# A third use for a spare weight place, and expert 30 in 4 MB transfers, in a mixture-of-experts block

## The reference

```python
def moe_ffn(xn, w_router, b_router, w_mlp1, b_mlp1, w_mlp2, b_mlp2):
    ...
    top_val, top_idx = lax.top_k(logits, TOP_K)
    gate = jax.nn.softmax(top_val, axis=-1)
    ...
    def expert_block(args):
        xb, e = args
        hdn = xb @ w_mlp1[e] + b_mlp1[e]
        glu = jnp.minimum(hdn[:, :D_FF], SWIGLU_LIMIT)
        lin = jnp.clip(hdn[:, D_FF:], -SWIGLU_LIMIT, SWIGLU_LIMIT)
        act = glu * jax.nn.sigmoid(SWIGLU_ALPHA * glu) * (lin + 1.0)
        return act @ w_mlp2[e] + b_mlp2[e]
    ...
    return jnp.einsum('tk,tkd->td', gate.astype(y.dtype), y).reshape(bsz, s, d)
```

## Time and profile before

| | |
|---|---|
| median of 3 runs | 1119.99 us (1119.98 to 1119.99) |
| profiled execution, own time | 1121.66 us |
| its span | 1119.8 us |
| PE busy | 1073.4 us, 96% of the span |
| DMA share of the span (SP's queue) | 93.2% |
| mean granted TensorE clock | 0.995 |
| moved | 439.15 MB, 392 GB/s over the span |
| items | 33 |
| 4 MB loads | 72 |

### The profile page before, as it was taken

One profiled execution on the slowest core, in us unless ns is written; L12 is line 12 of the kernel. 1 busy time (PEld: TensorE's weight loads), 2 busy tenths in 40 slices (PEclk: granted clock), 3 DMA queues, 4 the chain that ended last, 5 costly groups with the idle time before them and its releaser, 6 DMA issues.

```text
span 1119.8 us, 14338 instructions
## 1 busy us (share of the span) xinstructions
PE 1073.4 (96%) x5327; PEld 471.7 (42%) x5328; DVE 382.2 (34%) x852; ACT 247.1 (22%) x346; POOL 3.0 (0%) x12
## 2 busy tenths in 40 slices
PE   8999999999999999999889999999988889998996
PEld 8888888533333333333333333333333333332332
DVE  5987787422232222222222222222222222222223
ACT  5745674311111111110111111111111111111112
POOL 0000000000000000000000000000000000000000
PEclk9999999999999999999999999999999999999999
DMA  9755488999999999999999999999999999999996
GB/s 331 238 164 170 154 273 363 424 419 422 428 427 434 429 431 434 430 429 431 431 433 404 432 431 431 431 431 431 431 431 431 433 431 434 434 433 433 423 424 265
DMA packets 38309, 439.15 MB, mean 392 GB/s; under 512 B 5292, under 2 KB 5480, under 8 KB 22440
## 3 DMA queue, kind: packets, MB, share of 16 engines
q1 hardware_dynamic: 37776, 437.26, 93.2%
q10 hardware_dynamic: 504, 1.47, 0.5%
HBM read 437.67 MB, written 1.05 MB: 392 GB/s over the span
## 4 chain that ended last, share of the span: by engine, by line
PE 70%; DMA 26%; DVE 2%; ACT 2%; issue 0%; DVEq 0%; SPq 0%; PEldq 0%; ACTq 0%
PE bank L1162 29%; PE bank L1217 15%; DMA late_slots<-in_w_mlp_dram 14%; DMA ring<-in_w_mlp_dram 11%; PE bank L821 9%; PE bank L1064 4%; PE bank L815 2%; PE bank L1103 2%; PE bank L983 2%; PE bank L1031 2%; PE bank L1087 1%; ACT xn L716 1%; PE bank L1154 1%; DMA xs<-in_x_dram 1%; PE bank L1080 0%
## 5 line engine op out<-in xcount | busy, mean ns | idle before, releaser
L1162 PE MATMUL bank<-ring,xn 128*64 128x512 f32 x1232 | 280.0, 602 | 18.3 <-DMA ring<-in_w_mlp_dram 18.2
L1162 PE MATMUL bank<-late_slots,xn 128*64 128x512 f32 x880 | 197.9, 596 | 12.6 <-DMA late_slots<-in_w_mlp_dram 12.6
L1162 PEld LDWEIGHTS bank<-ring,xn 128*64 128x64 f32 x1232 | 85.1, 138 | 179.5 <-issue 152.4
L1217 PE MATMUL bank<-ring,smo 128*64 128x512 f32 x624 | 138.3, 595 | 0.0
L728 ACT ACTIVATE xn<-bank 128x512 f32<-128x512 f32 x33 | 19.7, 598 | 436.6 <-PE bank L1162 436.6
L1162 PEld LDWEIGHTS bank<-late_slots,xn 128*64 128x64 f32 x880 | 59.9, 136 | 126.6 <-issue 105.4
L1730 DVE SCALAR_TENSOR_TENSOR moe_y_lo<-bank,st,moe_y_hi 128x512 fp32r<-128x512 f32 x33 | 24.8, 751 | 235.5 <-ACT moe_y_hi L735 235.5
L1217 PE MATMUL bank<-late_slots,smo 128*64 128x512 f32 x416 | 92.1, 595 | 0.0
L1714 DVE TENSOR_SCALAR xn<-xn 128x512 f32<-128x512 f32 x33 | 14.1, 427 | 190.8 <-ACT xn L728 190.8
L1217 PEld LDWEIGHTS bank<-ring,smo 128*64 128x64 f32 x624 | 43.0, 137 | 81.0 <-issue 81.0
L735 ACT ACTIVATE moe_y_hi<-bank,st 128x512 fp32r<-128x512 f32 x33 | 22.7, 688 | 243.2 <-PE bank L1217 243.2
(11 more groups left out here) (278 smaller groups left out, 871.8 us busy)
## 6 DMA issues: line engine op xcount, KB each, us to landing
ring<-in_w_mlp_dram SPq DMA_DIRECT2D x43, 4096.0 KB, 37.6
late_slots<-in_w_mlp_dram SPq DMA_DIRECT2D x29, 4096.0 KB, 35.5
ring<-in_w_mlp_dram SPq DMA_DIRECT2D x28, 2048.0 KB, 14.8
late_slots<-in_w_mlp_dram SPq DMA_DIRECT2D x14, 2048.0 KB, 16.3
ring<-in_w_in_dram SPq DMA_DIRECT2D x22, 1024.0 KB, 5.6
late_slots<-in_w_mlp_dram SPq DMA_DIRECT2D x8, 1024.0 KB, 35.5
ring<-in_w_branch_dram SPq DMA_DIRECT2D x4, 1024.0 KB, 5.0
ring<-in_w_out_dram SPq DMA_DIRECT2D x4, 1024.0 KB, 7.0
```

The source lines that it names most:

```text
L1162: last = mm(B[4 + u][g * C:(g + 1) * C, :], xgT[:, k % 4, k // 4, :], by_group(held[k // 2][0][:, k % 2, u * FF:(u + 1) * FF], g), start=F ...
L1217: last = mm(B[7][g * C:(g + 1) * C, :], actT[:, j, h * C:(h + 1) * C], held[4 + h][0][:, j // 2, (j % 2) * D + g * N:(j % 2) * D + (g + 1) ...
```

## The change

`once` is now used three times, by chunks 5, 16 and 27 (`ONCE`). `place_of` counts the ten other places past them. The sequence of loads therefore goes round eleven places up to chunk 27: chunks 11 to 37 wait for the chunk eleven before them (each e of the new loop has its `freed` chunks and loads m = freed + 11), chunk 27's room is not loaded again, and from chunk 38 on each waits for the chunk ten before it, as before. The ten places shift by two numbers against the chunks. `QUADS` is 6 to 30 instead of 6 to 29, so that expert 30 comes in three 4 MB transfers instead of six of 2 MB. The matmuls are the same, on other addresses.

```diff
-QUADS = range(ROUND + 1, E - 2)
+QUADS = range(ROUND + 1, E - 1)
...
+ONCE = (CHUNKS - 1, CHUNKS - 1 + PLACES + 1, CHUNKS - 1 + 2 * (PLACES + 1))
+EXTRA_LAST = ONCE[-1]
...
+def place_of(m):
+
+    return None if m in ONCE else (m - sum(o < m for o in ONCE)) % PLACES
...
-            after = sp.value_load(first_item[0:1, 1:2], min_val=1, max_val=ITEMS - 1)
-            for i in range(CHUNKS - 1):
-                m = PLACES + 1 + i
-                if m != HALVED:
-                    wait_freed(after, i)
-                load(m // CHUNKS, m % CHUNKS, i)
...
-                        load(e - c + (m + PLACES) // CHUNKS, (m + PLACES) % CHUNKS, (m - 1) % PLACES, pieces(m + PLACES))
+                        load(e - c + (m + PLACES) // CHUNKS, (m + PLACES) % CHUNKS, (m - len(ONCE)) % PLACES, pieces(m + PLACES))
...
-                        load_quad(e + 1 if i == 1 else e + 2, (i // 2 + 2) % 3, (m - 2) % PLACES)
-
-            for e in range(1, ROUND + 1):
+                        load_quad(e + 1 if i == 1 else e + 2, (i // 2 + 2) % 3, (m - 1 - len(ONCE)) % PLACES)
+
+            for e in range((EXTRA_LAST + CHUNKS - 1) // CHUNKS):
+                after = sp.value_load(first_item[0:1, e + 1:e + 2], min_val=1, max_val=ITEMS - 1)
+                for i in range(CHUNKS):
+                    freed = CHUNKS * e + i
+                    m = freed + PLACES + (freed < EXTRA_LAST)
+                    if freed == EXTRA_LAST:
+                        continue
+                    if m // CHUNKS not in QUADS:
+                        if m != HALVED:
+                            wait_freed(after, i)
+                        load(m // CHUNKS, m % CHUNKS, place_of(m))
+                    elif m % 2:
+                        wait_freed(after, i)
+                        load_quad(m // CHUNKS, m % CHUNKS // 2, place_of(m - 1))
+
+            for e in range((EXTRA_LAST + CHUNKS - 1) // CHUNKS, ROUND + 1):
                 refill(e, e, CHUNKS, e + 2 in QUADS, e + 1 in QUADS)
```

More of the change, by code:

```diff
@@ L109, in constants @@
     return c
+ONCE = (CHUNKS - 1, CHUNKS - 1 + PLACES + 1, CHUNKS - 1 + 2 * (PLACES + 1))
+EXTRA_LAST = ONCE[-1]
+assert all(CHUNKS * e > EXTRA_LAST + PLACES - 2 for e in QUADS)
+def place_of(m):
+    return None if m in ONCE else (m - sum(o < m for o in ONCE)) % PLACES
 def landings():
@@ L116, in landings @@
         e, i = m // CHUNKS, m % CHUNKS
-        if m == CHUNKS - 1:
-            table.append(None)
+        place = place_of(m)
+        if place is None:
+            table.append((None, ONCE.index(m) + 1))
             continue
-        place = m if m < CHUNKS else (m - 1) % PLACES
         if e in QUADS and i % 2:
@@ L1122, in chunks @@
             def chunks(e):
-                return [(places[(CHUNKS * e + i - 1) % PLACES], place_landed[landing[CHUNKS * e + i][0]],
-                         landing[CHUNKS * e + i][1] * 16) for i in range(CHUNKS)]
+                held = []
+                for m in range(CHUNKS * e, CHUNKS * (e + 1)):
+                    place, count = landing[m]
+                    held.append((once[:, :, :] if place is None else places[place_of(m)],
+                                 once_landed if place is None else place_landed[place], count * 16))
+                return held
             def chunks_in_round(c, r):
@@ L1140, in chunks_in_round @@
                             assert 0 < need <= past[-1]
-                    held.append((places[(CHUNKS * c + i - 1) % PLACES], place_landed[place],
+                    held.append((places[place_of(CHUNKS * (ROUND + c) + i)], place_landed[place],
                                  r * (16 * step) + 16 * (last - step * len(at))))
@@ L1222, in _ @@
             with pe.Fori(0, after_first) as i:
-                item(i, [(places[n], place_landed[n], 16) for n in range(CHUNKS - 1)] + [(once[:, :, :], once_landed, 16)])
+                item(i, chunks(0))
             last_first = pe.value_load(first_item[0:1, E - 1:E], min_val=1, max_val=ITEMS - 1)
```

## The result

The changed kernel takes 1121.81 us (median of 15 runs, 1120.95 to 1122.78); the kernel before took 1119.71 beside it (15 runs, 1118.76 to 1120.84). The ratio is 1.0017, 95% interval 1.001 to 1.0024: 2.1 us slower. That is inside the range, 1118.4 to 1121.9, but a change of -0.1 us was forecast. The profiled execution took 1121.84, span 1119.9.

The account below looks back on a forecast made before the run. PE was taken to wait for weights, loading being slower by 3.2 us an expert. -1.8 (extra place) + 1.7 (expert 30) = -0.1 us took the profiled 1121.66 to 1121.5, less 1.67 to 1119.9; range 1118.4 to 1121.9.

Parts of the forecast that it names:

- What bounds the kernel: Over most experts: PE waits for weights, since loading is slower than PE by 3.2 us an expert.
- a shift of the stream carries through: From early loads to the end: 1.8 us gained early stays, as landings hold PE before and after the two-item expert.
- The extra place, -1.8: At chunks 16 and 17: earlier issue keeps the DMA engines from running dry, gaining 1.7 + 0.1 = 1.8 us.
- Nothing was lost there and nothing can be won: Around the two-item expert: DMA share falls to 0.71 in 596:602, but landings stay 9.8 us apart, so no gain.
- Expert 30, +1.7: At expert 30: 4 MB transfers make chunks usable only when their pair has landed, costing 1.7 us.
- the two waits named: At expert 30: PE waits 1.5 and 1.3 us, with no wait at expert 31.
- The low clock, rival 1: At expert 30's first wait: a granted clock of 0.50 may follow; total +0.4, 1120.4 us; chance 0.20.
- Rival 2: At chunk 17: one held-up DMA engine makes the gap, so the place gains nothing; 1121.7 us, slower by 0.15%; chance 0.17.
- The slip of 1.5: At the load issued at 424.1: landings 11.3 us apart instead of 9.7, queue full, untouched by the extra place.
- rival 3: In the early loads: a deeper queue also removes the 1.5 us at the landing of 456.6; 1118.4 us; chance 0.11.
- Rival 4: At expert 30: each transfer pays its fixed cost, so three fewer are 7.2 us faster; 1112.8 us; chance 0.02.

Follow-up runs that it names:

- e3: The kernel before, unchanged, run again for a second profile: median 1119.95 us, ratio 1.0003; profiled execution 1119.23.
- e11: The kernel before, unchanged, profiled a third time: 1119.12 us in one execution.
- e5: The changed kernel with its new places but without the extra depth (chunks 16 to 37 wait as before): 1121.23 us against 1119.60 for the kernel before, ratio 1.0017.
- e13: The changed kernel with the extra depth for chunks 16 to 23 alone: 1122.82 us in one execution, against 1120.48 for the kernel before.
- e14: The changed kernel with the extra depth for chunks 24 to 37 alone: 1121.20 us in one execution, against 1120.48 for the kernel before.
- e15: Second profile of the changed kernel with the extra depth for chunks 16 to 23 alone: 1122.45 us in one execution, against 1120.48 for the kernel before.
- e16: Second profile of the changed kernel with the extra depth for chunks 24 to 37 alone: 1120.93 us in one execution, against 1120.48 for the kernel before.
- e1: The changed kernel with expert 30 in six 2 MB transfers as before (expert 1's chunk 3 in halves): 1119.92 us against 1119.64 for the kernel before, ratio 1.0000.
- e2: The kernel before with only expert 30 put in three 4 MB transfers: 1121.22 us against 1119.64, ratio 1.0016.
- e6: The kernel before with expert 30's chunk 3 loaded ahead of chunk 2, both still 2 MB: 1122.58 us against 1119.60, ratio 1.0031.
- e7: The kernel before with expert 30's chunk 1 loaded ahead of chunk 0, both still 2 MB: 1121.94 us against 1119.60, ratio 1.0017.
- e8: The kernel before with expert 30's chunk 5 loaded ahead of chunk 4, both still 2 MB: 1124.17 us against 1119.60, ratio 1.0038.

## Why the prediction was wrong

**What bounds the kernel, and that a shift of the stream carries through.** Right. PE waits for the stream before and after the expert with two items; for one order of the last loads and one clock "closing" is the same to 0.05 us however late expert 29's weights land.

**The extra place, -1.8.** This is the step that failed, in two ways. Its mechanism at chunk 17 was right: the DMA engines run short there, the change stops it, and only the depth for chunks 16 to 23 does it (the change's depth reaches chunk 37, not 35). Its size came from one execution. The 1.7 us were 0.4 and 0.2 in the other two profiles of the kernel before, and 0.2 to 1.7 in the eleven profiles without the early depth, with a median of 0.7; with it they are 0.2 at most. The profiled execution's 1121.66 was also above all 15 runs of the comparison. The prediction saw that it lay 1.67 above the median and subtracted 1.67 at the end, as if it were the profiler's cost; the changed kernel's profiled execution, 1121.84, lies 0.03 from its median, so profiling costs nothing like that. The excess of its span over those of e3 and e11, 2.6 us, is 1.5 ahead of expert 0's chunk 2 (188.0 against 186.6 and 186.4) and 1.7 in the loads (842.0 against 840.2 and 840.4), less 0.6 in the rest. Most of the 1.7 was the very gap that the prediction then counted as a gain: about 1.4 was taken off twice.

The second failure is the sentence on the expert with two items, "Nothing was lost there and nothing can be won". The landings of the kernel before lost nothing, but only because their last completions made up a stall that moved the first ones by 3.7 us (13.4 instead of 9.7 apart). With the depth for chunks 16 to 23 the next transfer lands 1.3 to 2.0 us late. That the one brings the other is shown by e5 and by e13 to e16; why the last completions then make up less was not shown. Net, the depth is worth 0.3 and 0.6 us in the wrong direction by the medians (e1 over before, changed over e5), both inside their intervals: no gain that lasts, and no loss that is proved.

**Expert 30, +1.7.** Right in mechanism and size: 74.89 - 73.18 = 1.71, at the two waits named, and e2 alone is 1.6 over before. The lateness of a pair's first chunk is the cause (closing stretches of e6 to e8, clock set apart).

**The low clock, rival 1.** It occurs at expert 30's first chunk in e2, e5 and e13, and makes the closing stretch 0.5 longer each time, but not in the three profiles of the change.

**Rivals 2 to 4.** Rival 2, the slower side, is where the result fell. Its condition, "less than about 1.7 us are gained early", held. Its reason, one held-up engine, was half of it: in the profile before, the last completion of chunk 17 came 1.7 late and the first 0.5, so some of the gap was a dry spell for all and the rest a few falling behind. But the extra place did remove the whole of it there, and the loss came back later. It gave 1121.7 and 1121.81 was measured. The slip of 1.5 that rival 3 hoped away is gone from its place, but one like it, of 1.1 to 1.5, stands some 50 us earlier, at the 4 MB load issued at 379, in every profile with the early depth. Rival 4 found nothing for it.

**The account of the 2.1.** Closing +1.7. Loads +1.2 (841.5 against the 840.3 of e3 and e11). Rest -0.6, because in e3 and e11 PE waits once more inside the last 32 matmuls (0.48 in e3, 6.23 + 1.08 us in two pieces), for a last load that landed 2.5 and 2.3 us after the one before it; in the change, and in the first profile of the kernel before, that is 1.2, and PE does not wait. Together +2.3 by profiles, 2.1 by medians. The medians of e1 and e2, +0.3 and +1.6, add up to 1.9. The first profile of the kernel before is left out of this sum: it lay above all 15 runs. With it as a third the terms are loads +0.7 and rest -0.4. Nor are the +1.2 all due to the depth: the three kernels with the new places and no early depth (e5, e14, e16) stand at 841.3 to 841.4 too. What makes those late was not tested.

That the spans of the first two profiles are equal comes out of the same terms: closing +1.7, the landing of expert 0's chunk 2 -1.4, loads -0.3.

The row of that last wait in e3:

```profile
1106.63 1.08 PE L1217 MATMUL bank<-late_slots,smo 128*64 128x512 f32 x4 [0.48 <-DMA late_slots<-in_w_mlp_dram]
```

No version beat the kernel before: e1 is level with it.

## What to carry to other kernels

When the profiled execution lies outside the spread of the runs, look for the excess in its trace before counting any gap as something to be won, and take a second profile: here one gap of 1.7 us was counted that two more executions of the same kernel had at 0.2 and 0.4. Where PE and a stream of loads run neck and neck, a larger transfer costs the wait for its first half, wherever the slack is less than that; three 4 MB transfers cost 1.7 us for the 0.2 they saved. A starved moment removed early is a gain only if no later stall hands it back. And a landing is the last of sixteen completions: even landings do not show that nothing was lost.

## What the runs showed that was not expected

A wait of 3.1 to 3.3 us at expert 30 brought the clock to 0.50 both times (e6, e8) and cost 1.7 and 2.7 us more than the wait itself; waits of 1.8 to 1.9 brought it in some executions and not in others, for the same instructions at the same place (e2 and e5 with, the changed kernel three times without).

The landings of back-to-back transfers keep their distance of 9.7 us for hundreds of microseconds and then jump by up to 2.0 at a few places. With the early depth the places are the same in each profile (issues at 379 and 596, 7 of 7); in the kernel before they are not (424 in its first profile, 333 and 351 in e3, 313 and 379 in e11). At 379 the DMA share stays near 1 and the first completion of the transfer is on time (9.7); only the last is late.

Most jumps go with an instruction fetch. The page has a queue for these, 22 of 16 KB in an execution, each of some 1.1 us:

```profile
q8 instruction: 22, 0.36, 0.1%
```

In the 18 traces 1800 loads landed between 190 and 1000 us. For 311 of them a fetch began after the previous landing or up to 2 us ahead of it. 74 landed over 0.3 us later than a full queue's distance (2.49 for 1 MB, 4.90 for 2 MB, 9.72 for 4 MB), and 65 of these are among the 311; the other nine are chunk 17 of e3 and the eight late landings behind the expert with two items. So a fetch goes with nearly every slip but those at the stall, the one at 379 included (a fetch at 397 to 398 in all seven). That it causes them was not tested, and it is a rival for the size of the gap at chunk 17, where one began between 249 and 253 in every profile.
